# Turned query and key banks evicted whole and split from SBUF, keys of the second half projected first, position bias loaded one projection later

## The reference

```python
def diff_attention(q, k, v, lam):              # q, k already RMS-normed per 64-wide head
    q = q * (dk ** -0.5)
    for i in range(S // Q_BLOCK):              # 4 blocks of 128 queries
        ...
        s = jnp.einsum('bqhjd,bkhjd->bhjqk', qb, kb) - slopes * dist
        s = jnp.where(dist >= 0, s, -jnp.inf)
        p = jax.nn.softmax(s, axis=-1)
        a = p[:, :, 0] - lam * p[:, :, 1]
        outs.append(jnp.einsum('bhqk,bkhe->bqhe', a, vb))
```

## Time and profile before

| | us |
|---|---|
| median of 3 runs | 917.53 |
| lowest to highest | 916.22 to 918.62 |
| the profiled execution's own time | 916.43 |
| its span in the profile | 914.6 |
| TensorE busy | 894.0 |
| VectorE, ScalarE, GpSimd busy | 438.2, 404.7, 440.7 |
| DMA | 89.70 MB, mean 98 GB/s |
| mean granted TensorE clock | 0.996 |

### The profile page before, as it was taken

The page is one execution under the profiler, slowest core; times in us unless marked ns, Lnnn a source line. Parts: engine busy times, 40 slices in busy tenths (PEclk is TensorE's granted clock), DMA queues, the critical chain, the costliest instruction groups (busy, mean ns, idle before and its releaser), DMA issues.

```text
span 914.6 us, 12681 instructions
## 1 busy us (share of the span) xinstructions
PE 894.0 (98%) x4648; PEld 726.3 (79%) x4648; DVE 438.2 (48%) x981; ACT 404.7 (44%) x880; POOL 440.7 (48%) x376
## 2 busy tenths in 40 slices
PE   9999999999999999998989999999989998999998
PEld 7877888888888888877878888889868766777776
DVE  3211262545104424667586555546627866553631
ACT  4533322433233354554655443344435684655531
POOL 4544435444446645654434344545348472234362
PEclk9999999999999999999999999999999999999999
DMA  8433122323323263243433243333533322011113
GB/s 311 153 89 104 54 68 92 93 71 101 105 92 92 93 183 106 81 116 96 134 92 93 71 147 109 107 106 82 120 97 86 111 74 65 24 48 47 47 47 115
DMA packets 46126, 89.70 MB, mean 98 GB/s; under 512 B 4928, under 2 KB 6720, under 8 KB 46064
## 3 DMA queue, kind: packets, MB, share of 16 engines
q1 hardware_dynamic: 44576, 88.34, 32.3%
q10 hardware_dynamic: 1488, 0.55, 0.2%
HBM read 78.36 MB, written 2.12 MB: 88 GB/s over the span
## 4 chain that ended last, share of the span: by engine, by line
PE 80%; DVE 9%; issue 4%; POOL 3%; DMA 2%; ACT 1%; SPq 0%; ACTq 0%; DVEq 0%; POOLq 0%
PE Z L1767 22%; PE Z L1769 21%; PE Z L1768 21%; PE A L1954 3%; PE A L1963 2%; PE A L1992 2%; PE A L1886 2%; DVE z_sb L1279 2%; DMA rms_dram<-rms 1%; POOL w_lo L983 1%; PE A L1937 1%; DVE rstd L1182 1%; PE A L1902 1%; PE A L1777 1%; PE A L1874 1%
## 5 line engine op out<-in xcount | busy, mean ns | idle before, releaser
L983 POOL TENSOR_TENSOR w_lo<-raw,w_hi 128x512 fp32r<-128x512 f32 (+1 forms) x262 | 346.6, 1330 | 444.4 <-ACT w_hi L609 443.7
L609 ACT CAST w_hi<-raw 128x512 fp32r<-128x512 f32 (+1 forms) x262 | 157.7, 614 | 287.6 <-PE Z L1769 263.0
L1767 PE MATMUL Z<-w_hi,hT_hi 128*128 128x512 f32 (+1 forms) x544 | 217.4, 400 | 3.1 <-POOL w_lo L983 3.0
L1769 PE MATMUL Z<-w_hi,hT_lo 128*128 128x512 f32 (+1 forms) x544 | 211.8, 389 | 0.0
L1768 PE MATMUL Z<-w_lo,hT_hi 128*128 128x512 f32 (+1 forms) x544 | 211.4, 389 | 0.0
L1767 PEld LDWEIGHTS Z<-w_hi,hT_hi 128*128 128x128 f32 x544 | 102.7, 189 | 24.0 <-POOL w_lo L983 3.7
L1769 PEld LDWEIGHTS Z<-w_hi,hT_lo 128*128 128x128 f32 x544 | 102.5, 188 | 20.9
L1768 PEld LDWEIGHTS Z<-w_lo,hT_hi 128*128 128x128 f32 x544 | 102.8, 189 | 18.1
L1767 PE MATMUL Z<-hT_hi,w_hi 128*128 128x512 f32 x260 | 113.1, 435 | 0.4 <-DVE hT_lo L1214 0.4
L1769 PE MATMUL Z<-hT_hi,w_lo 128*128 128x512 f32 x260 | 102.3, 394 | 0.0
L1768 PE MATMUL Z<-hT_lo,w_hi 128*128 128x512 f32 x260 | 101.8, 391 | 0.0
(11 more groups left out here) (243 smaller groups left out, 1351.3 us busy)
## 6 DMA issues: line engine op xcount, KB each, us to landing
raw<-in_w_in SPq DMA_DIRECT2D x91, 512.0 KB, 3.6
k_stack<-keys_once SPq DMA_DIRECT2D x32, 256.0 KB, 4.2
raw<-in_w_out SPq DMA_DIRECT2D x16, 512.0 KB, 3.5
raw<-in_ret_w_o SPq DMA_DIRECT2D x8, 512.0 KB, 3.3
raw<-in_diff_w_o SPq DMA_DIRECT2D x8, 512.0 KB, 3.3
x_sb<-in_x SPq DMA_DIRECT2D x4, 512.0 KB, 5.6
x_sb<-in_xT SPq DMA_DIRECT2D x4, 512.0 KB, 6.1
out<-x_sb SPq DMA_DIRECT2D x8, 256.0 KB, 2.6
```

Of the source, the lines that this page charges most:

```text
L609: act.copy(w_hi[:, s % SPLIT_SLOTS, 0:width], raw[:, c % RAW_SLOTS, s - CHUNK_START[c], 0:width]).then_inc(hi_ready, 1)
L983: pool.tensor_tensor(w_lo[:, s % SPLIT_SLOTS, 0:width], raw[:, c % RAW_SLOTS, s - CHUNK_START[c], 0:width], w_hi[:, s % SPLIT_SLOTS, 0:wid ...
L1767: pe.matmul(out, l_hi, r_hi, start=first, stop=False)
L1769: return pe.matmul(out, l_lo, r_hi, start=False, stop=last)
```

## The change

Four things are edited. (1) ScalarE evicts a turned bank whole, as scaled fp32, into one of two new tiles (`q_once`, `k_once`), and counts it in `qk_out`; the high part is then copied from there, and VectorE subtracts there, too. `turn_probs` waits for `qk_out` in place of `q_lo` or `k_lo`. `queries_low` moves to the end of step a of i = 2, `keys_low` into step a of i = 1, ahead of the copy L1464. (2) Group 14 projects keys and group 15 queries, and every head's keys are turned ahead of its queries (before, heads 0 and 4 had queries first). (3) `diff_due` has one slope after slot 115; the sums of squares come at slots 4, 7, 9, 11 in place of 2, 4, 6, 8; the first output norm moves from slabs 5 and 6 of group 17 to slabs 1 and 2 of group 18; one entry of KEYS_SPREAD moves. (4) The first two bias loads move from slab 4 of group 25 to slab 4 of group 26 (G_CT).

```diff
-        g += [("w_in", 3072 + 1024 * j + 512 * i, 512, KD, "copy", 1024 * j + 512 * i) for j in range(3)]
+        g += [("w_in", 3072 + 1024 * j + 512 * i, 512, KD, "copy", 1024 * j + 512 * i) for j in ((1, 0, 2) if i else range(3))]
-HEAD_NORM = {10: 0, 11: 1024, 14: 512, 15: 1536, 25: 0, 26: 512}
+HEAD_NORM = {10: 0, 11: 1024, 14: 1536, 15: 512, 25: 0, 26: 512}
-DIFF_FIRST, DIFF_SECOND, DIFF_THIRD, DIFF_LAST = 16, 116, 130, 208
+DIFF_FIRST, DIFF_SECOND, DIFF_LAST = 16, 116, 208
...
-    if v < DIFF_THIRD:
-        return 34 + 5 * (v - DIFF_SECOND + 1) // (DIFF_THIRD - DIFF_SECOND)
-    return min(86, 39 + 47 * (v - DIFF_THIRD + 1) // (DIFF_LAST - DIFF_THIRD))
+    return min(86, 34 + 52 * (v - DIFF_SECOND + 1) // (DIFF_LAST - DIFF_SECOND))
...
-    return 2 * w + 1 + (1 - i if keys_first(w) else i)
-KEYS_SPREAD = {8: 0, 12: 1, 20: 2, 28: 3, 36: 4, 40: 5, 44: 6, 48: 7}
+    return 2 * w + 2 - i
+HEAD_SUMS = {4: 0, 7: 1, 9: 2, 11: 3}
+KEYS_SPREAD = {8: 0, 14: 1, 20: 2, 28: 3, 36: 4, 40: 5, 44: 6, 48: 7}
...
-                for p, at in enumerate(((G_LAYER2 + 1, 4), (G_LAYER2 + 1, 4), (G_GATES, 4), (G_GATES + 1, 0))):
+                for p, at in enumerate(((G_CT, 4), (G_CT, 4), (G_GATES, 4), (G_GATES + 1, 0))):
...
             def diff_queries(w):
                 act.wait_ge(qk_t, turn_count(w, 0))
+                if w:
+                    act.wait_ge(q_lo, 2 * w)
+                act.activation(q_once[:, :], diff_qk_bank(w, 0)[:, :], ACT.Copy, scale=cols[:, 35:36]).then_inc(qk_out, 1)
+                act.wait_ge(qk_out, turn_count(w, 0))
                 if w >= 2:
                     act.wait_ge(s_mm, 8 * (w - 1))
                 for j, half in enumerate(halves):
-                    act.activation(q_stack[half, stack_slot(w, j), :], diff_qk_bank(w, 0)[half, :], ACT.Copy,
-                                   scale=cols[half, 35:36]).then_inc(q_hi, 1)
+                    act.copy(q_stack[half, stack_slot(w, j), :], q_once[half, :]).then_inc(q_hi, 1)
             def diff_keys(w):
                 act.wait_ge(qk_t, turn_count(w, 1))
                 if w:
+                    act.wait_ge(k_lo, w)
+                act.activation(k_once[:, :], diff_qk_bank(w, 1)[:, :], ACT.Copy, scale=cols[:, 36:37]).then_inc(qk_out, 1)
+                act.wait_ge(qk_out, turn_count(w, 1))
+                if w:
                     act.wait_ge(k_in, 64 * w)
-                act.activation(keys_once[:, 0, :], diff_qk_bank(w, 1)[:, :], ACT.Copy,
-                               scale=cols[:, 36:37]).then_inc(k_hi, 1)
+                act.copy(keys_once[:, 0, :], k_once[:, :]).then_inc(k_hi, 1)
...
+                    if i == 1 and h + 1 < H:
+                        keys_low(h + 1)
                     if 0 <= n - LAG < N:
...
+                    if i == 2 and h + 1 < H:
+                        queries_low(h + 1)
                     yield
                     if i in (0, 1) and h + 1 < H:
                         yield
-                        (keys_low if keys_first(h + 1) == (i == 0) else queries_low)(h + 1)
...
-                    dve.scalar_tensor_tensor(q_stack[halves[1 - j], slot, :], diff_qk_bank(w, 0)[half, :],
-                                             cols[half, 35:36], q_stack[half, slot, :], ALU.mult,
-                                             ALU.subtract).then_inc(q_lo, 1)
+                    dve.tensor_tensor(q_stack[halves[1 - j], slot, :], q_once[half, :], q_stack[half, slot, :],
+                                      ALU.subtract).then_inc(q_lo, 1)
...
-                dve.scalar_tensor_tensor(keys_once[:, 1, :], diff_qk_bank(w, 1)[:, :], cols[:, 36:37], keys_once[:, 0, :],
-                                         ALU.mult, ALU.subtract).then_inc(k_lo, 1)
+                dve.tensor_tensor(keys_once[:, 1, :], k_once[:, :], keys_once[:, 0, :], ALU.subtract).then_inc(k_lo, 1)
...
-                    if normed_in(g) and 2 <= TT * k + t <= 8 and t % 2 == 0:
-                        head_sums(2 * k + t // 2 - 1, squares_d)
+                    if normed_in(g) and TT * k + t in HEAD_SUMS:
+                        head_sums(HEAD_SUMS[TT * k + t], squares_d)
...
-                    if g == G_DIFF0 + 4 and k in (5, 6):
+                    if g == G_DIFF0 + 5 and k in (1, 2):
                         next(norms["first"])
...
-                    pe.wait_ge(head_normed, 12 + 4 * i)
+                    pe.wait_ge(head_normed, 16 - 4 * i)
...
-                        if keys_first(job + 1) == (mi == 0):
-                            pe.wait_ge(k_lo, job + 2)
-                        else:
-                            pe.wait_ge(q_lo, 2 * job + 4)
+                        pe.wait_ge(qk_out, 2 * (job + 1) + mi + 1)
...
-                        diff_turn(h + 1, 1 - i if keys_first(h + 1) else i)
+                        diff_turn(h + 1, 1 - i)
```

More of the change, by code:

```diff
@@ L116, in diff_due @@
         return 34 * (v - DIFF_FIRST + 1) // (DIFF_SECOND - DIFF_FIRST)
-    if v < DIFF_THIRD:
-        return 34 + 5 * (v - DIFF_SECOND + 1) // (DIFF_THIRD - DIFF_SECOND)
-    return min(86, 39 + 47 * (v - DIFF_THIRD + 1) // (DIFF_LAST - DIFF_THIRD))
-def keys_first(w):
-    return w % 4 != 0
+    return min(86, 34 + 52 * (v - DIFF_SECOND + 1) // (DIFF_LAST - DIFF_SECOND))
 def turn_count(w, i):
-    return 2 * w + 1 + (1 - i if keys_first(w) else i)
-KEYS_SPREAD = {8: 0, 12: 1, 20: 2, 28: 3, 36: 4, 40: 5, 44: 6, 48: 7}
+    return 2 * w + 2 - i
+HEAD_SUMS = {4: 0, 7: 1, 9: 2, 11: 3}
+KEYS_SPREAD = {8: 0, 14: 1, 20: 2, 28: 3, 36: 4, 40: 5, 44: 6, 48: 7}
 RET_SLAB = SLAB0[G_RET0]
@@ L285, in build @@
             keys_once = sb("keys_once", [P, 2, S], F32R, scope)
-            sb("sgd_middle", [P, 2, S], F32, scope)
+            q_once = sb("q_once", [P, S], F32, scope)
+            k_once = sb("k_once", [P, S], F32, scope)
             q_stack = sb("q_stack", [P, 4, S], F32R, scope)
@@ L372, in build @@
         r_xe, q_latent = sem("r_xe"), sem("q_latent")
-        qk_t, bias_r = sem("qk_t"), sem("bias_r")
+        qk_t, qk_out, bias_r = sem("qk_t"), sem("qk_out"), sem("bias_r")
         q_hi, q_lo, k_hi, k_lo, k_in = sem("q_hi"), sem("q_lo"), sem("k_hi"), sem("k_lo"), sem("k_in")
@@ L779, in diff @@
                     if i in (0, 1) and h + 1 < H:
-                        (diff_keys if keys_first(h + 1) == (i == 0) else diff_queries)(h + 1)
+                        (diff_queries if i else diff_keys)(h + 1)
                         yield
@@ L871, in diff_slot @@
                 if g == G_DIFF0 and k == 1:
+                    diff_keys(0)
                     diff_queries(0)
-                    diff_keys(0)
                 if g + 1 in TURNED and k >= 4:
@@ L1503, in diff_slot @@
                 if g == G_DIFF0 and k == 1:
+                    keys_low(0)
                     queries_low(0)
-                    keys_low(0)
                 for t in range(TT):
-                    if normed_in(g) and 2 <= TT * k + t <= 8 and t % 2 == 0:
-                        head_sums(2 * k + t // 2 - 1, squares_d)
+                    if normed_in(g) and TT * k + t in HEAD_SUMS:
+                        head_sums(HEAD_SUMS[TT * k + t], squares_d)
                     for _ in range(diff_due(v + t) - diff_due(v + t - 1)):
@@ L1846, in diff_turn @@
                 c0 = 1024 * i + P * w
-                at = turn_count(w, i) - turn_count(w, 0 if w % 4 == 0 else 1)
+                at = 1 - i
                 if 4 * w - 5 + at > 0:
@@ L1850, in diff_turn @@
                 elif at and w:
-                    pe.wait_ge(k_lo, 2)
+                    pe.wait_ge(qk_out, 3)
                 if w == H // 2:
-                    pe.wait_ge(head_normed, 12 + 4 * i)
+                    pe.wait_ge(head_normed, 16 - 4 * i)
                 for t in range(TT):
@@ L2074, in project @@
                         pe.wait_ge(head_normed, 8)
+                        diff_turn(0, 1)
                         diff_turn(0, 0)
-                        diff_turn(0, 1)
                     if k == 5 and g == G_VALUES:
```

## The result

The changed kernel is slower: 921.14 us against 916.22 us in the median, ratio 1.0047 (95% interval 1.0028 to 1.0066). On a second chip the same two kernels gave 1.0062 (1.0048 to 1.0075). The median of the kernel before is now one of seven runs, where the forecast started from 917.53 in three: forecast was 2.3 us less, to 915.2 (between 911.0 and 919.5), and measured are 4.9 us more. The profiled execution took 921.62 us with a span of 919.8, 5.2 more than before; by the terms of the sum it should have been 912.25.

A forecast was written before the change was run, and what follows sets the result against it. TensorE's 20.6 us of standing still was taken to bound the kernel, chiefly its waits for VectorE. The terms 0.35 + 1.4 + 2.8 - 0.5 - 1.7 gave 2.35 us less, 915.2 us in the median, range 911.0 to 919.5.

The forecast's parts named there:

- The first step: What bounds the kernel: only time TensorE stands still matters, 20.6 us of 914.6, led by transposes waiting for low halves.
- The wait at 420: Head 4's transpose waits for the norm: 3.1 us (2.3 to 4.5) for 2.58, loss 0.5 plus 1.7 low clock.
- the one at 391: Low-key wait of 1.84 us goes; some 0.4 us left at the next transpose, 1.5 if held; gain 1.4.
- the four old waits: TensorE's attention waits near 380, 391, 420 and 470 us, whose terms were 0.35, 1.4, -0.5 - 1.7 and 2.8 us.
- the 0.35 us goes: Wait at 380 us behind the third sum of squares; that sum comes after the attention step, gaining 0.35 us.
- rival C: Slower: GpSimd holds the SBUF subtractions where VectorE sets the end; 3.7 us more, 921.2; chance 0.12.
- 1.3 back at step 60: Scores wait for VectorE's maxima behind the gate products; 1.3 us returns after the wait at 470, net gain 2.8.
- 0.5 for 0.5: Key wait of 0.5 us from the first output norm, which moves and meets head 7's turn: counted as even.
- At 517, nothing: Outputs' wait late in the attention: the forecast's sum has no term for it.
- ScalarE's 1.4 us a head: Extra ScalarE operations for keys and queries, at most 1.4 us a head, 11 us in all, costed at nothing.
- B: TensorE's waits only move to the next thing VectorE owes, at full price; about 1.2 us more, 918.7; chance 0.15.
- A: The waits go and are not replaced, since VectorE has time to catch up; 5.8 us less, 911.7; chance 0.35.

The follow-up runs named there:

- low_early: Changed kernel with the low subtractions alone put back to their old place, the end of step c; ratio 1.0036 to the kernel before.
- order_due: order_only plus the changed kernel's due times alone; ratio 1.0015 to the kernel before.
- norm_back: Changed kernel with the first output norm alone put back to slabs 5 and 6 of group 17; ratio 1.0029 to the kernel before.
- due_back: Changed kernel with the due times alone back to those of the kernel before; ratio 1.0026 to the kernel before.
- evict_only: Kernel before with the new eviction alone, low subtractions and schedule in their old places; ratio 1.0003 to the kernel before.
- order_only: Changed kernel with low subtractions, norm, sums and due times of before; new eviction, keys-first order, bias and spread entries stay; ratio 0.9970 to the kernel before.
- sums_back: Changed kernel with the sums of squares alone back at slots 2, 4, 6, 8; ratio 1.0059 to the kernel before.
- with the holds: evict_only plus bias move, with head 4's first turns later: 0.9963; also turns at the gate's end held behind its products: 0.9924 to the kernel before.

## Why the prediction was wrong

The first step held: TensorE's idle time is the whole question, and L1902's waits went. The wait at 420 came as written (3.1 forecast, 3.16 measured, low clock at it in this profile, none in the second), and the one at 391 lay within its bounds (0.4 to 1.5 forecast, 1.28 measured), but by luck, as is said below. The step that failed is the price of the new order: the later place of the low subtractions, the new due times and the moved norm were costed at nothing or at a gain, because only the four old waits were followed along VectorE's queue. Term by term against the profile after:

- **At 380, "the 0.35 us goes": 1.47 stands there, 1.5 us off.** I followed the low queries to 420 and 470 but not to head 2's turn. They now come at the end of a step a, ahead of two sums and the maxima. With step c order the wait is gone (low_early), so the new place is its cause. Some 1.0 us of it is the hold of rival C: 2.38 us for two subtractions of 0.69.
- **At 470, "1.3 back at step 60": 1.20 + 1.53 came back, 1.4 us off.** The gain of the new due times that I counted there is a loss by itself (order_due: 2.33 + 0.37 + 2.20 us of waits for 2.05). I had the low queries ahead of the gate products (473.36), but costed only the scores' wait for the maxima; the first tile of the next group waits for its bank, freed by those products, before that.
- **At 488, "0.5 for 0.5": 1.86 us and a low clock, 3.1 us off.** The moved norm keeps VectorE busy to 488.75, and the low keys take another 0.69 ahead of the copy. norm_back removes both wait and drop.
- **At 517, nothing: 1.61 where 0.5 was, 1.1 us off.** One slot earlier, step 79 falls behind VectorE's fourth product over group 19's banks (L1326, x4). Undoing the due times alone gives 0.50 (due_back).
- **ScalarE's 1.4 us a head "at nothing": 0.74 us at 343, 0.6 off.** Two copies from `q_once` stand ahead of the gate's tanh, and the bank is free later:

```profile
340.93 1.26 ACT L757 CAST q_stack<-q_once 64x512 fp32r<-64x512 f32 x2
342.21 1.26 ACT L637 ACTIVATE tmp<-Z,rms 128x512 f32<-128x512 f32 x2
```

Before, this wait was 0.15 us, with no copy in that place; evict_only has 0.74 as well, so it belongs to the eviction.
- **391: 1.28 for 0.4, 0.9 off.** The upper bound of 1.5 stood for a low subtraction that is held, and this one was not (0.68 us at 396.09). Nor were the products slower than before: four took 3.47 us, three 2.98 in the earlier trace rows. They began 2.7 us later (391.95 for 389.27), while TensorE came 1.7 us later (396.15 for 394.44); what made VectorE later by that one microsecond was not tested.
- **At 672: 2.35 for 2.98**, 0.6 us better.

Together 1.5 + 1.4 + 3.1 + 1.1 + 0.6 + 0.9 - 0.6 = 8.0 us, against 919.8 - 912.25 = 7.6 that were missing. The sum closes, but each term is a difference of single profiles, and they act on one another. order_only is 2.7 us below the kernel before, near the 2.3 forecast, and that is luck: 2.0 us of it are low clock, which the forecast took off at 470 and put back at 426, and it lacks the due times that were to bring the gain at 470. From it to the changed kernel, place, due times, sums and norm take back 7 to 8.4 us (0.9970 to 1.0047 or 1.0062, on three chips).

Of the rivals, B is nearest: the waits moved to the next thing VectorE owes. Its +1.2 us was too small because I priced it at the four old waits and gave new ones no place. A fell: VectorE's 121 of 207 busy us say nothing of a place where three bursts meet. Its price was also too small for its own words: a full removal would have taken away the 3.1 us at 426 as well. C is a part only: the median of L1496 is 687 ns against 684 at best, and the holds lie mostly off the path, but the one at 377 is on it. The Trainium skill's page "SBUF — State Buffer", section "Who interferes with whom", has a rule of this kind (the one who issues first keeps the port); the trace agrees at 376.93, where two subtractions that take 2 x 0.684 us at best took 2.38, beside GpSimd's w_lo from 376.58 to 378.05, which had started first. The bias move was nothing, as said.

Low clock is a part of the loss that the profiles alone would give wrongly, as one stretch more or less in an execution is 1.7 us. By the clocks of all runs it is 1.2 of the 5.5 us on the second chip; on the first, where only the profiled execution of the kernel before has its clock on record, it stays open. What decides whether a given wait is followed by it stays open, too.

## What to carry to other kernels

When a wait is removed by letting its owner finish later, list what now stands behind the deferred work on its in-order engine at every turn of the loop, not only at the turns where the old wait was. Due times that fall on the end of a projection's gate or a norm decide more than the dependency: with the same new eviction, what stands where on VectorE and the due times moved the ratio from 1.0062 to 0.9908. Parts of one change that share a wait should be priced by adding them to a clean kernel; undone one by one in the full change, the sums looked free and the norm cost up to 3 us, while with the low parts in step c the norm cost nothing in time. And a time should be split into idle time and low clock before it is explained: over all runs the two moved against each other in low_early and sums_back, and together in order_only and with the holds.

## What the runs showed of the hardware

The drop of TensorE's clock is not fixed by the length of a wait. In the 18 profiled executions, each of the 18 drops in the attention stretch began within 2 us of the end of a wait of at least 1.86 us, or in it; 11 other waits as long as that had none. The wait of 3.16 us at one instruction had a drop to 0.50 in the changed kernel's first profile and full clock (1.00) in its second. The four kernels without a drop there had no wait above 2.05 us, and two of them none above 1.1. A drop lasted 3.4 us, once 6.8 (at 2.78 us, sums_back). A forecast should weigh it at such a wait by these counts, not take it as certain; the two kernels without any such wait lost 0.0 and 0.2 us a run to low clock.

The small write `rms_dram` took 13.71 us before and 13.09 after:

```profile
658.66 13.09 DMA rms_dram<-rms
```

On the first chip the wait that it causes was 2.98 and 2.35 us; in the profiles on the four other chips it was 0 to 1.7 us. The same kernel, the changed one, had 2.35 us on the first chip and 0.40 on the second, in one profile each.
